# The joined expert stage: low parts of the first block moved from GpSimd to VectorE, two blocks turned first, the closing sums spread over three engines

## The reference, cut to what matters

```python
# first block (EXPERTS 16), then the last line of it
for e in range(N_EXPERTS):
    he = jax.nn.silu(t @ exp_w1[e]) * (t @ exp_w3[e])
    y = y + comb[:, e:e + 1] * (he @ exp_w2[e])
...
h = h + hier_moe(...)
return rms_norm(h[:, N_META:], final_g)
# second block (EXPERTS 32)
def expert_block(args):
    xb, e = args
    hb = jax.nn.silu(xb @ w_gate[e]) * (xb @ w_up[e])
    return hb @ w_down[e]
```

## Time and profile before

| what | value |
| --- | --- |
| median of three runs | 3196.64 us (3192.37 to 3198.96) |
| profiled execution | 3206.02 us, its span 3204.3 us |
| PE, DVE, ACT, POOL busy | 85%, 49%, 34%, 27% of the span |
| mean granted TensorE clock | 0.915 of full speed |
| first expert stage | about 1046 us to 1407 us |
| second expert stage | about 2754 us to 3204 us |

### The profile page before, as it was taken

One profiled execution on the slowest core, in us unless ns is written; L12 is line 12 of the kernel. 1 busy time (PEld: TensorE's weight loads), 2 busy tenths in 40 slices (PEclk: granted clock), 3 DMA queues, 4 the chain that ended last, 5 costly groups with the idle time before them and its releaser, 6 DMA issues. The chain is left out here.

```text
span 3204.3 us, 33977 instructions
## 1 busy us (share of the span) xinstructions
PE 2716.4 (85%) x11990; PEld 2013.1 (63%) x11990; DVE 1572.0 (49%) x1841; ACT 1088.7 (34%) x1435; POOL 856.7 (27%) x743
## 2 busy tenths in 40 slices
PE   5898997999979499719899699988999979499994
PEld 3897555767758477517655355546767757377773
DVE  4294341222232678661166444433643563578886
ACT  3012331000011377530133344431332131267773
POOL 1232331221211345303000233313322312244542
PEclk8999798999989699959799799998999989699997
DMA  3111112111132599844222233322111114479998
GB/s 88 34 46 24 30 33 55 53 39 39 33 119 99 193 377 361 327 173 144 99 59 60 69 78 80 80 51 68 40 39 46 46 49 144 165 269 345 347 341 315
DMA packets 220933, 404.99 MB, mean 126 GB/s; under 512 B 41657, under 2 KB 160777, under 8 KB 198057
## 3 DMA queue, kind: packets, MB, share of 16 engines
q1 hardware_dynamic: 203560, 370.21, 34.4%
q0 software_dynamic: 17280, 33.59, 2.8%
HBM read 351.97 MB, written 76.68 MB: 134 GB/s over the span
## 5 line engine op out<-in xcount | busy, mean ns | idle before, releaser
L1890 DVE TENSOR_TENSOR moe_run_w_low_up<-moe_run_w,moe_run_w_high_up 128x2048 fp32r<-128x2048 f32 x112 | 256.5, 2291 | 108.2 <-ACT moe_run_w_high_up L1726 76.7
L1726 ACT CAST moe_run_w_high_up<-moe_run_w 128x2048 fp32r<-128x2048 f32 x116 | 221.2, 1907 | 120.3 <-DMA moe_run_w<-w_gate 56.3
L134 PE MATMUL rnn_ps<-uT_again_high,rnn_w_high 128*128 128x512 f32 x512 | 205.4, 401 | 35.5 <-POOL rnn_w_low L147 19.5
L1672 PE MATMUL moe_run_up<-moe_run_w_high_up,moe_run_xT_high 128*128 128x512 f32 x464 | 195.6, 422 | 23.6 <-issue 13.6
L134 PE MATMUL rnn_ps<-uT_again_low,rnn_w_high 128*128 128x512 f32 x512 | 202.8, 396 | 0.0
L134 PE MATMUL rnn_ps<-uT_again_high,rnn_w_low 128*128 128x512 f32 x512 | 202.7, 396 | 0.0
L134 PE MATMUL merge_gates<-uT_high,merge_wg_high 128*128 128x512 f32 x384 | 170.7, 445 | 17.8 <-POOL merge_wg_low L147 17.8
L1672 PE MATMUL moe_run_up<-moe_run_w_high_up,moe_run_xT_low 128*128 128x512 f32 x464 | 185.3, 399 | 0.0
L1672 PE MATMUL moe_run_up<-moe_run_w_low_up,moe_run_xT_high 128*128 128x512 f32 x464 | 185.3, 399 | 0.0
L1200 DVE TENSOR_TENSOR merge_gated<-merge_branch,merge_gate 128x512 f32<-128x512 f32 x48 | 33.2, 692 | 303.7 <-ACT merge_gate L1185 303.7
L1048 ACT ACTIVATE mla_probs<-mla_scores 128x512 f32<-128x512 f32 x192 | 94.2, 491 | 197.2 <-PE mla_scores L985 142.4
(11 more groups left out here) (465 smaller groups left out, 6893.2 us busy)
## 6 DMA issues: line engine op xcount, KB each, us to landing
moe_run_w<-exp_w SPq DMA_DIRECT2D x72, 1024.0 KB
moe_run_w<-w_gate SPq DMA_DIRECT2D x34, 1024.0 KB
moe_run_w<-w_up SPq DMA_DIRECT2D x34, 1024.0 KB
moe_run_w<-w_down SPq DMA_DIRECT2D x34, 1024.0 KB
rnn_raw<-w_in SPq DMA_DIRECT2D x32, 512.0 KB, 3.9
merge_raw<-w_in SPq DMA_DIRECT2D x24, 512.0 KB, 3.9
norm_x<-x SPq DMA_DIRECT2D x16, 512.0 KB, 5.1
out_h<-x SPq DMA_DIRECT2D x16, 512.0 KB, 6.5
```

The costliest lines, as they stand in the source:

```text
L134: last = pe.matmul(out, a, b, start=(k == 0), stop=(k == n - 1))
L1672: last = pe.matmul(up[p][:], a, w, start=(h == 0 and k == 0), stop=(h == 1 and k == 3 * HK - 1))
L1726: act.copy(hi[p][j], raw[p][j][:]).then_inc(s_hi[j], 1)
L1890: dve.tensor_tensor(lo[p][j], raw[p][j][:], hi[p][j].bitcast(F32), ALU.subtract).then_inc(s_lo[j], 1)
```

## The change

1. GpSimd's two subtractions (L1579) and the semaphores `s_pre` go. VectorE makes these low parts as `rest(0, 0, 0)` and `rest(0, 0, 1)`, right behind the list of blocks. The order of VectorE's other low parts changes with it, and SyncE's loads wait on `s_lo` throughout.
2. VectorE's differences for the softmax (`ex`, `gx`) are made while TensorE counts; the three operations on `along` go from ahead of the count to behind the one-hot tables.
3. TensorE turns both first blocks ahead of the first products.
4. At the end of the first stage ScalarE weights the first result (into `y[t % 2]`), GpSimd adds it to `h[t]`, VectorE adds the second; mean and scaled result of earlier tiles are written between them (`NT + 2` rounds). In the second stage VectorE still does both sums.

```diff
-        s_pre = st.sem_n("first_low_ready")
...
-                        if p == 0 and j < 2:
-                            sp.wait_ge(s_pre[j], 1)
-                        else:
-                            sp.wait_ge(s_lo[j], p + 1)
+                        sp.wait_ge(s_lo[j], p + 1)
...
-                for j in range(2):
-                    pool.wait_ge(s_hi[j], 1)
-                    pool.tensor_tensor(lo[0][j], raw[0][j][:], hi[0][j].bitcast(F32),
-                                       ALU.subtract).then_inc(s_pre[j], 1)
...
+                if g_row is not None:
+                    for t in range(NT):
+                        pool.wait_ge(s_h[t], 16)
+                        pool.wait_ge(s_weighted, t + 1)
+                        pool.tensor_tensor(h[t], h[t], y[t % 2][:], ALU.add).then_inc(s_first, 1)
...
                 turn_rows(0, 0, True)
+                turn_rows(0, 1, True)
                 up_half(0, 0, 0, True)
                 up_half(0, 0, 1, True)
-                turn_rows(0, 1, True)
...
-                    for t in range(NT):
-                        act.wait_ge(s_sum, 2 * t + 2)
-                        act.activation(junk, h[t], ACT.Square, accum_out=ss[:, t:t + 1]).then_inc(s_ss, 1)
-                        act.wait_ge(s_ms, t + 1)
-                        act.activation(rt[:, t:t + 1], ms[:, t:t + 1], ACT.Sqrt).then_inc(s_rt, 1)
+                    act.wait_ge(s_weights, 1)
+                    for t in range(NT + 1):
+                        if t < NT:
+                            act.wait_ge(s_yk[t], 32)
+                            if t >= 2:
+                                act.wait_ge(s_first, t - 1)
+                            act.mul(y[t % 2][:], yk[t][0], weights[:, 0, t:t + 1]).then_inc(s_weighted, 1)
+                        if t:
+                            act.wait_ge(s_sum, t)
+                            act.activation(junk, h[t - 1], ACT.Square, accum_out=ss[:, t - 1:t]).then_inc(s_ss, 1)
+                            act.wait_ge(s_ms, t)
+                            act.activation(rt[:, t - 1:t], ms[:, t - 1:t], ACT.Sqrt).then_inc(s_rt, 1)
...
-                for j in range(2):
-                    dve.sem_inc(s_lo[j], 1)
-
...
+                rest(0, 0, 0)
+                rest(0, 0, 1)
+                rest_of_rows(0, 0)
                 rest(0, 1, 0)
-                TT(ex[:], v2[:], v1[:], ALU.subtract)
-                TT(gx[:], lg, wide(gmax[:], NG), ALU.subtract).then_inc(s_diff, 1)
+                rest_of_rows(0, 1)
+                rest(0, 1, 1)
                 rest(0, 0, 2)
-                rest_of_rows(0, 0)
-                rest(0, 1, 1)
-                rest_of_rows(0, 1)
                 gated(0, 0, True)
...
+                def weighted(t, k):
+                    return STT(out=h[t], in0=yk[t][k], scalar=weights[:, k, t:t + 1], in1=h[t], op0=ALU.mult, op1=ALU.add)
+
+                def mean_of(t):
+                    dve.wait_ge(s_ss, t + 1)
+                    TS(ms[:, t:t + 1], ss[:, t:t + 1], 1.0 / D, EPS, ALU.mult, ALU.add).then_inc(s_ms, 1)
+
+                def scaled(t):
+                    dve.wait_ge(s_rt, t + 1)
+                    dve.reciprocal(inv[:, t:t + 1], rt[:, t:t + 1]).then_inc(s_inv, 1)
+                    if t == 0:
+                        dve.wait_ge(s_g, 16)
+                    dve.wait_ge(s_inv, t + 1)
+                    STT(out=h[t], in0=h[t], scalar=inv[:, t:t + 1], in1=g, op0=ALU.mult, op1=ALU.mult).then_inc(s_out, 1)
...
+                else:
+                    for t in range(NT + 2):
+                        if t < NT:
+                            dve.wait_ge(s_yk[t], 32)
+                            dve.wait_ge(s_first, t + 1)
+                            weighted(t, 1).then_inc(s_sum, 1)
+                        if 1 <= t <= NT:
+                            mean_of(t - 1)
+                        if t >= 2:
+                            scaled(t - 2)
```

More of the change, by code:

```diff
@@ L1830, in _ @@
                 TT(both, oh[:, 0], oh[:, 1], ALU.add).then_inc(s_both, 1)
-                own(dve.tensor_reduce(odd[:], cst["ident"][:].rearrange("p (c two) -> p two c", two=2)[:, 1, :], AX.X,
-                                      ALU.add))
+                TT(ex[:], v2[:], v1[:], ALU.subtract)
+                TT(gx[:], lg, wide(gmax[:], NG), ALU.subtract).then_inc(s_diff, 1)
+                dve.tensor_reduce(odd[:], cst["ident"][:].rearrange("p (c two) -> p two c", two=2)[:, 1, :], AX.X,
+                                  ALU.add)
                 dve.wait_ge(s_const, 6)
-                own(TS(along[:], odd[:], -1.0, 0.5, ALU.mult, ALU.add))
-                own(TT(along[:], along[:], s_id[:], ALU.mult))
-                own(STT(out=along[:], in0=odd[:], scalar=-0.5, in1=along[:], op0=ALU.mult, op1=ALU.add))
                 dve.wait_ge(s_rank, 1)
@@ L1871, in _ @@
                     dve.sem_inc(s_hot, 1)
+                own(TS(along[:], odd[:], -1.0, 0.5, ALU.mult, ALU.add))
+                own(TT(along[:], along[:], s_id[:], ALU.mult))
+                own(STT(out=along[:], in0=odd[:], scalar=-0.5, in1=along[:], op0=ALU.mult, op1=ALU.add))
                 own(STT(out=sb_at[:], in0=odd[:], scalar=blocks, in1=along[:], op0=ALU.mult, op1=ALU.add))
@@ new lines, in _ @@
+                if g_row is None:
+                    for t in range(NT):
+                        dve.wait_ge(s_h[t], 16)
+                        dve.wait_ge(s_yk[t], 32)
+                        own(weighted(t, 0))
+                        weighted(t, 1).then_inc(s_sum, 1)
+                else:
+                    for t in range(NT + 2):
+                        if t < NT:
+                            dve.wait_ge(s_yk[t], 32)
+                            dve.wait_ge(s_first, t + 1)
+                            weighted(t, 1).then_inc(s_sum, 1)
+                        if 1 <= t <= NT:
+                            mean_of(t - 1)
+                        if t >= 2:
+                            scaled(t - 2)
```

30 lines of the change are left out of this document (7 added, 23 removed).

## The result

| | kernel before | changed kernel |
| --- | --- | --- |
| median, same chip | 3195.41 us (3192.37 to 3198.96, 4 runs) | 3163.34 us (3157.36 to 3166.08, 4 runs) |
| profiled execution, span | 3206.02, 3204.3 us | 3157.36, 3155.6 us |
| mean granted TensorE clock | 0.915 | 0.923 |

The ratio is 0.9897 (95% interval 0.9878 to 0.9915): 32.1 us faster, where 26.2 were forecast. The forecast time was 3170.4 us. Now and then a kernel here runs 45 to 80 us longer than in its other executions, in the two traces that caught it (`old_end`, `down_part_early`) ahead of the first expert stage, and the ratios leave such executions out.

What follows compares the result with a forecast made beforehand. The prediction took transfers to bound the loop over blocks and serial chains of engines the front and end. Gains of 12.95 us (first stage) and 13.2 (second), together 26.2, gave 3170.4 us from 3196.64, with 3157 to 3182 for 8 in 10.

Steps and rivals of the forecast that it cites:

- the round of waits: End of the first stage: weighting, add, sum, mean and root wait on each other in turn, 5.5 us a tile.
- the likeliest case: Whole kernel: the forecast itself, 3170.4 us with its own range of 3162 to 3178, chance 0.64.
- list, first and second stage: Front: without GpSimd's subtractions VectorE reaches the list of blocks 7.85 and 8.5 us earlier.
- gather: Front: rows of x land earlier as weight loads are released later, 1 us a stage, bounds nothing and 4.
- first two blocks: First two blocks: turning block 1 ahead of the first products gains 3.6 us in the first stage, 3.7 in the second.
- end of the first stage: End of the first stage: overlapping the engines over tiles gains 0.5 us, bounds 7 lost and 2.5 won.
- nothing changes: Front: rival that the 4.47 us have another cause than GpSimd, so VectorE's outliers stay; chance 0.02.
- the pass count: First two blocks: TensorE's reading of it before block 1 costs an estimated 0.55 us, bounds 0.2 and 2.
- Later loads: Behind the front: SyncE's third to fifth loads move later, costed at nothing, with a margin of 3 us.
- given back: First blocks: rival that they wait for weights or pass count, gain only 12 to 17 us; chance 0.18.
- slower than before: Weight loads: rival that the late loads cost more than 13 us a stage; chance 0.03.
- the end overlaps: End of the first stage: rival that waits do not limit it, 5 to 17 us more won; chance 0.08.

Runs made afterwards that it cites:

- old_end: The changed kernel without its new end of the first stage (sums as before): 3152.67 and 3157.90 us, ratio 0.985.
- down_part_early: The changed kernel, but VectorE makes block 0's down low part third, so the third weight load is released earlier: 3215.18 us, one run.
- pool_later: The kernel before, but GpSimd makes its first two low parts behind the first two gathers: 3159.61 to 3173.02 us, ratio 0.989.
- change_again: The changed kernel itself, run once more in a later set (the repeat): 3158.81 us, ratio 0.9919 against the kernel before.
- weighting_ahead: The changed kernel, but at the end ScalarE weights the first result two tiles ahead: 3150.45 us, one run.
- gather_first: The changed kernel, but VectorE's first two low parts wait for a semaphore GpSimd raises behind the first gather: 3162.81 us, one run.

## Why the prediction was right, and where its sizes were off

The mechanism was right in the front, the blocks and the round of waits at the end, and right in sign for the gather. The time came out 7 us lower, within the likeliest case's own range, as three terms were too small; 1.2 of the 7 are the median of the kernel before, which was 3195.41 in the comparison and not 3196.64. By the marks:

| term | forecast | measured |
| --- | --- | --- |
| list, first and second stage | 7.85, 8.5 | 7.86, 8.57 |
| gather | 1, 1 | 2.24, 2.27 |
| first two blocks | 3.6, 3.7 | 4.2, 1.7 to 5.1 |
| end of the first stage | 0.5 | 2.8 |
| sum | 26.2 | 29.6 to 33.1 |

The sum agrees with the 32.1 us of the first comparison. The 27 us of the second lie below it, but its interval (0.9905 to 0.9933, 21 to 30 us) still reaches it.

- **Front.** Right to a tenth. Four outliers, each ending with a subtraction, were enough to price the whole; `pool_later` shows that only the overlap mattered. The rival that nothing changes falls.
- **Gather.** The sign and the reason were right, loads that come later, but I took "nearer to nothing" because one load still overlaps. That a load overlaps costs the wait for the first packet, which did not change (3.18 and 3.15 us); the gain is in the part behind it, where the loads beside the rows fell from 1.38 to 0.41 MB. That the third load no longer meets the gather fits the bytes of before; no run isolates it. The descriptor work of the first stage got 0.3 us longer (2.75 to 3.06), where I said that it stays, but it began 0.3 us earlier and ended at the same distance behind the list, 3.72 us.
- **Blocks.** First products 6.02 us behind the turn (forecast 6.4), 4 slow ones (3.5), block 1 at 12.5 (13.2), `turn_middle` at 15.3 (15.9). Nearly all of the 0.6 us missed is the pass count: I gave its reading 0.55 us, which no row showed, and it shows no gap. I took the clock to rise at the same moment as before, and 4 slow products came out as forecast; that was partly luck, since the repeat has 3 and 9. In the second stage I took one trace's 20.10 us for a fixed number; it holds a fall of the clock that other executions of the same order do not have.
- **Later loads.** ScalarE makes the high parts of the second pair without a wait of a microsecond; its first wait for weights behind the front is this, in its timeline of the changed kernel:

```profile
1107.46 1.91 ACT L1721 CAST moe_run_w_high_up<-moe_run_w 128x2048 fp32r<-128x2048 f32 x1 [0.99 <-DMA moe_run_w<-exp_w]
```

  So "given back" and "slower than before" fall. That transfers pace the loop was not shown by the row that I read it from: in the same 100 us TensorE is busy 93.66. The forecast needed only that the loop keeps its length. Over all runs the loop takes 238 to 242 and 340 to 347 us, in no order that follows the kernels; the 3 and 5 us by which it is shorter in the first trace of after are not the change's, as `change_again` has 239.59 and 346.74.
- **End.** The round of waits was the right bound, but 5.21 us and not 5.5: the estimate of 5.4 had some 0.2 too much in handing over, and the 0.1 for a meeting with the scaling did not occur, as it ends (1351.92) when the add starts (1351.88). Over 7 tiles that is 2 of the 2.3 us missed. The exclusion, weighed in the prediction as a bound of 5.0 us a tile, binds, with what is left of the round, as soon as the round is cut. Its bound is lower than 5.0, though: when they follow each other these instructions take 2.20 (add), 1.07 and 1.09 us, not the 2.41, 1.30 and 1.28 of their own rows, together 4.36 beside the 4.59 us a tile of `weighting_ahead`. The rival "the end overlaps" needed the round to be absent, and the round was there.
- **Range.** The lower bound of 15.5 us does not follow from its own terms: 7.85 + 8.5 + 0 + 5 - 5 is 16.35, and with the 7 us that the end's own bound allows it would be 14.35. The bounds of the single terms that are given add up to 34.2 at the top, not 36. The result lies inside either way.

For the rule of the Trainium skill (SBUF — State Buffer, Who interferes with whom), that a VectorE instruction with two SBUF inputs and a GpSimd instruction that reads SBUF exclude each other: the runs agree at three new places (5.80 instead of 2.29, 3.35 instead of 1.28, and 3.29 instead of 2.34 on GpSimd's side).

What stays open: why the clock rises 7.2 us behind the turn in one execution and 10.4 in another, why the gather's first packet waits 3.1 us beside any load, and why the loop and the start of the stages vary by some us between executions.

## What to carry to other kernels

An operation that is ten times as long as its equals on one engine may be a collision: look at what the other engine ends at the same moment, and move that work to where its neighbour waits anyway. Before sharing a serial end among engines, write down its round of waits; tiles overlapped on the one engine that was already fastest (3.97 us a tile) beat three engines in a round (5.21). Cut the time of a small transfer at its first packet before pricing it: loads under way can hold up its start and its course separately. Where a stretch of TensorE differs between executions, count the products at either level of the clock before looking for another cause. And read a gain of some tens of us between marks inside the stage, not from two spans.

## What the runs showed of the hardware

- GpSimd's descriptor work for a gather stretches beside VectorE's subtraction of two SBUF tensors: 3.06 us beside it, 1.22 and 1.10 with VectorE waiting, 2.17 again where a later one meets it.
- A semaphore that GpSimd raises behind a gather can be raised before its descriptors are made (`gather_first`), so it cannot order other work behind them.
- A gather of 0.4 MB needs 3.2 us from its descriptors' end without other loads (0.70 to its first packet, 2.52 behind it), 5.13 with 1.41 MB of loads beside it (3.15 and 1.98), and 7.38 with 2.71 MB beside it (3.18 and 4.20).
- After the same pause of TensorE, about 2.5 us, the granted clock fell in one execution (0.56) and stayed at 1.00 in another.
- Behind the same work of TensorE the granted clock rose from 0.50 to 1.00 between 7.15 and 10.43 us after the first turn, over the traces of the change's order with its loads as they are; the first two blocks took 14.97 to 16.48 us with it.
